# Delta rule scan: right sides solved by halves of a chunk in opposite quadrants, another order of masks, key products and preparation

## The reference

```python
decay = exp(where(tril, gcum[:, None] - gcum[None, :], -inf))
kb    = k * beta[:, None]
lower = where(strict, (kb @ k.T) * decay, 0)
rhs   = concat([v * beta, kb * exp(gcum)], -1)
u, w  = triangular_solve(I + lower, rhs)        # unit lower triangular
attn  = where(tril, (q @ k.T) * decay, 0)
# the state S is carried from chunk to chunk
v_new = u - w @ S
o     = (q * exp(g)) @ S + attn @ v_new
S     = S * exp(g_last) + (k * exp(g_last - g)).T @ v_new
```

## Time and profile before

| what | value |
|---|---|
| median of 3 runs | 4209.52 us (4208.9 to 4209.89) |
| the profiled execution's own time | 4206.61 us |
| its span | 4204.9 us |
| TensorE busy (PE) | 3783.0 us, 90% |
| VectorE busy (DVE) | 2123.8 us, 51% |
| ScalarE busy (ACT) | 870.1 us, 21% |
| GpSimd busy (POOL) | 397.5 us, 9% |

### The profile page before, as it was taken

How to read it: one execution, slowest core, us unless ns; L and a number is a source line. 1 busy time by engine, 2 the same in 40 slices (tenths; PEclk the granted TensorE clock), 3 DMA queues, 4 the chain that set the end, 5 groups by cost and what they waited for, 6 DMA issues and landing times. The chain is left out here.

```text
span 4204.9 us, 67380 instructions
## 1 busy us (share of the span) xinstructions
PE 3783.0 (90%) x28350; PEld 2482.9 (59%) x28350; DVE 2123.8 (51%) x4187; ACT 870.1 (21%) x2114; POOL 397.5 (9%) x506
## 2 busy tenths in 40 slices
PE   6988988995999978889799598897989999999998
PEld 3477467772444435565677243334358878468877
DVE  3777677555222215576646433333364455564455
ACT  3244134411000002251621100002230001441001
POOL 0033013100111110150600000000000000000000
PEclk8999999997999989999999799998999999999999
DMA  6510520026999971211411799994112222122221
GB/s 234 180 38 12 180 92 18 21 81 268 394 393 391 401 260 41 89 54 40 141 61 61 281 404 403 405 421 158 48 66 81 70 90 83 53 81 98 77 90 55
DMA packets 166941, 674.21 MB, mean 160 GB/s; under 512 B 13480, under 2 KB 26984, under 8 KB 142064
## 3 DMA queue, kind: packets, MB, share of 16 engines
q1 hardware_dynamic: 155232, 650.89, 40.6%
q0 software_dynamic: 9984, 16.78, 1.8%
q10 hardware_dynamic: 1424, 2.23, 0.1%
HBM read 652.85 MB, written 17.02 MB: 159 GB/s over the span
## 5 line engine op out<-in xcount | busy, mean ns | idle before, releaser
L3744 PE MATMUL bank<-weight_ring_extra_b,xs_b 128*32 128x512 f32 x2544 | 281.8, 594 | 2.4 <-DMA weight_ring_extra_b<-in_moe_in 2.4
L3744 PE MATMUL bank<-weight_ring,xs_b 128*32 128x512 f32 x1936 | 220.1, 605 | 12.4 <-DVE xs_b L3847 6.2
L2853 PE MATMUL bank<-heads_out_b,swiglu_sums_b 128*128 128x256 f32 x1008 | 224.5, 379 | 0.0
L3836 ACT ACTIVATE moe_silu_b<-bank 128x256 f32<-128x256 f32 x80 | 25.5, 383 | 960.4 <-PE bank L3744 960.4
L3847 DVE TENSOR_SCALAR xs_b<-bank,factor_b,mod_b 128x64 f32<-128x64 f32 (+1 forms) x384 | 95.6, 328 | 229.1 <-PE bank L3728 229.1
L2853 PEld LDWEIGHTS bank<-heads_out_b,swiglu_sums_b 128*128 128x128 f32 x1008 | 191.9, 190 | 25.7
L3744 PEld LDWEIGHTS bank<-weight_ring_extra_b,xs_b 128*32 128x32 f32 x2544 | 79.2, 110 | 178.3 <-issue 173.2
L3801 PE MATMUL bank<-weight_ring_extra_b,moe_hidT_b 128*32 128x256 f32 x2784 | 160.8, 390 | 11.1 <-DMA weight_ring_extra_b<-in_moe_down 9.6
L3888 DVE TENSOR_TENSOR heads_out_b<-heads_out_b,bank 128x256 f32<-128x256 f32 x256 | 90.3, 416 | 154.0 <-PE bank L3781 154.0
L1764 POOL TENSOR_TENSOR d_level_b<-d_low_b,d_mask_b 128x256 f32<-128x256 f32 x144 | 115.5, 830 | 551.1 <-DVE d_far_b L2023 548.2
L2237 PE MATMUL bank<-hT_b,token_block_sums_b 128*128 128x256 f32 x608 | 145.1, 393 | 15.7 <-DVE hT_b L2371 15.7
(11 more groups left out here) (618 smaller groups left out, 7614.2 us busy)
## 6 DMA issues: line engine op xcount, KB each, us to landing
weight_ring_extra_b<-in_moe_in SPq DMA_DIRECT2D x60, 2048.0 KB, 23.4
weight_ring<-in_moe_in SPq DMA_DIRECT2D x48, 2048.0 KB, 24.6
weight_ring_extra_b<-in_moe_down SPq DMA_DIRECT2D x33, 2048.0 KB, 25.2
weight_ring<-in_ada_w SPq DMA_DIRECT2D x24, 2048.0 KB, 8.0
weight_ring<-in_moe_down SPq DMA_DIRECT2D x21, 2048.0 KB, 25.3
weight_ring<-in_ssd_w_in SPq DMA_DIRECT2D x12, 2048.0 KB, 8.2
hT_b<-in_moe_in SPq DMA_DIRECT2D x10, 2048.0 KB, 41.8
weight_ring<-in_ffn_w_gate SPq DMA_DIRECT2D x10, 2048.0 KB, 8.0
```

The source lines that it names most:

```text
L2853: last = pe.matmul(out, lhs[:, k, :], rhs[:, k, :], start=(k == 0), stop=(k == HK - 1))
L3744: last = pe.matmul(in_bank(g)[lanes[c], :], xs[:, e % 2, kt, g * GROUP:(g + 1) * GROUP], w[:, k, :, c * COLS:(c + 1) * COLS], start=(kt == 0),
```

## The change

- Level 64 is dropped. The two 64x64 inverses of a chunk are used directly: the half of the chunk that comes first in a direction's order is solved (`early`), its result is multiplied with `far` (`carry`) and subtracted from the other half's right side (`rest`), and that half is solved (`late`). First half for the forward direction is rows 0 to 63, for the backward one rows 64 to 127, so the products of the two directions lie in opposite quadrants of the array and are issued in turns. Each round is cut in two by heads (r = 0: heads 0 and 2, r = 1: heads 1 and 3).
- After level 32, VectorE's subtraction becomes eight `scalar_tensor_tensor` operations of 128x64, which also multiply with beta, from a copy scaled beforehand (`UB`). The multiplication of `R` with beta and that of `far` with beta are gone. `far` is one buffer whose halves belong to the two directions.
- Keys with queries of the next step go to bank 0 and stand in TensorE's stream before the solve; the transposed keys come after the level-1 transposes and into the same bank. Both Grams of the next step stand after the solve and before the outputs. The outputs go to bank 3, the state sums to bank 2.
- On VectorE both `lower` calls of the next step stand after the forward state and before the backward output. The queries are scaled beside level 8 instead of 16.
- On GpSimd the attention masks stand before the block of level 16 instead of before that of level 4.
- Six more semaphores for the moved products and the preparation.

```diff
@@ order of marks @@
-    PEM = ["gram", "qk", "kturn", "ks", "turn1"]
-    for s in LEVELS[1:]:
+    PEM = ["ks", "turn1", "kturn"]
+    for s in SMALL[1:]:
...
-    PEM += ["new", "o", "state"]
-    BESIDE = {2: ["rest"], 4: ["kend"], 8: ["rb"], 16: ["qs"]}
+    PEM += ["early0", "early1", "carry0", "carry1", "late0", "late1", "o", "state"]
+    BESIDE = {2: ["rest"], 4: ["kend"], 8: ["qs"], 16: ["scaled"]}
@@ GpSimd @@
                 for n, size in enumerate(SMALL):
-                    if n == 2:
+                    if n == 4:
                         attention(s)
@@ TensorE @@
+            def keys_with_queries(d, s):
+                cols = slice(chunk_cols(ORDER[d][s]), chunk_cols(ORDER[d][s]) + P)
+                if s:
+                    wait(pe, dvm[d], s - 1, "kend")
+                else:
+                    wait(pe, acm[d], s, "rowexp")
+                for h in range(GQ):
+                    last = pe.matmul(B[d][0][:, h, :], kT[:, h, cols], qT[:, h, cols], start=True, stop=True)
+                last.then_inc(qk_done[d], 1)
+            def solve(s):
+                for r in range(2):
+                    for d in (FWD, BWD):
+                        wait(pe, dvm[d], s, f"inverse{r}")
+                        wait(pe, dvm[d], s, "rest")
+                    for h in (r, r + 2):
+                        for d in (FWD, BWD):
+                            early, _ = early_late(d)
+                            last = pe.matmul(B[d][1 + r][early, h, :], UW[early, d, 0, h, :], R[early, d, h, :], start=True,
+                                             stop=True)
+                            if h == r + 2:
+                                last.then_inc(pem[d].sem, 1)
...   (carry: far[early] with NW[early] into rows late, after ScalarE's early{r};
...    late: UW[late] with R[late] into rows late, after VectorE's rest{r})
+                if s + 1 < TT:
+                    for d in (FWD, BWD):
+                        keys_with_queries(d, s + 1)
+                solve(s)
+                if s + 1 < TT:
+                    for d in (FWD, BWD):
+                        gram(d, s + 1)
                 for d in (FWD, BWD):
-                    wait(pe, dvm[d], s, "rb")
-                    wait(pe, dvm[d], s, f"uv{TOP}")
-                    each(d, s, "new", B[d][1], lambda h: U[:, d, h, :], lambda h: R[:, d, h, :])
...
+                    for r in range(2):
+                        wait(pe, acm[d], s, f"late{r}")
+                        for h in (r, r + 2):
+                            pe.matmul(B[d][3][:, h, :], QS[:, d, h, :], S[:, d, h, :], start=True, stop=False)
+                            last = pe.matmul(B[d][3][:, h, :], AT[:, d, h, :], NW[:, d, h, :], start=False, stop=True)
                     last.then_inc(pem[d].sem, 1)
-                    each(d, s, "state", B[d][3], lambda h: KE[:, d, h, :], lambda h: NW[:, d, h, :])
-                    if s + 1 < TT:
-                        gram(d, s + 1)
+                    each(d, s, "state", B[d][2], lambda h: KE[:, d, h, :], lambda h: NW[:, d, h, :])
@@ ScalarE @@
+                for n, part in enumerate(("early", "late")):
+                    for r in range(2):
+                        for d in (FWD, BWD):
+                            wait(act, pem[d], s, f"{part}{r}")
+                            if s and n == 0:
+                                wait(act, pem[d], s - 1, "state")
+                            rows = early_late(d)[n]
+                            act.activation(by_two(NW[rows, d])[:, :, r, :], solved_bank(d, r)[rows], ACT.Copy, scale=-1.0) \
+                                .then_inc(acm[d].sem, 1)
@@ VectorE @@
-                dve.tensor_tensor(far[rows], far[rows], beta[rows], ALU.mult).then_inc(dvm[d].sem, 1)
...
+                for r in range(2):
+                    for d in (FWD, BWD):
+                        wait(dve, pem[d], s, f"uv{SMALL[-1]}")
+                        wait(dve, dvm[d], s, "scaled")
+                        for h in (r, r + 2):
+                            at = h0 + h
+                            last = dve.scalar_tensor_tensor(out=UW[:, d, 0, h, :], in0=small_bank(d, 1 + r)[:, h // 2, :],
+                                                            scalar=dec.beta[:, t, d, at:at + 1], in1=UB[:, d, h, :],
+                                                            op0=ALU.mult, op1=ALU.subtract)
+                        last.then_inc(dvm[d].sem, 1)
+                for r in range(2):
+                    for d in (FWD, BWD):
+                        _, late = early_late(d)
+                        wait(dve, pem[d], s, f"carry{r}")
+                        mine = by_two(R[late, d])[:, :, r, :]
+                        dve.tensor_tensor(mine, mine, solved_bank(d, r)[late], ALU.subtract).then_inc(dvm[d].sem, 1)
                 for d in (FWD, BWD):
                     t = ORDER[d][s]
+                    if d == BWD and s + 1 < TT:
+                        for e in (FWD, BWD):
+                            lower(e, s + 1)
                     wait(dve, pem[d], s, "o")
...
-                    if s + 1 < TT:
-                        lower(d, s + 1)
```

More of the change, by code:

```diff
@@ L1781, in turned @@
             def turned(d, s, size):
[L1783 to L1790, removed]
+                for pair in range(GQ // 2):
+                    both = slice(2 * pair, 2 * pair + 2)
+                    last = pe.transpose(small_bank(d, 3)[:, both, :].rearrange("p h c -> p (h c)"),
+                                        UW[:, d, 0, both, :].rearrange("p h c -> p (h c)"), core.ident[:])
                 last.then_inc(pem[d].sem, 1)
@@ L1833, in _ @@
                     cols = slice(chunk_cols(ORDER[d][s]), chunk_cols(ORDER[d][s]) + P)
[L1834 to L1845, removed]
                     if s:
@@ L1856, in _ @@
                     else:
-                        wait(pe, acm[d], s - 1, "new")
+                        wait(pe, acm[d], s - 1, "late0")
                     for h in range(GQ):
@@ L1862, in _ @@
                     last.then_inc(pem[d].sem, 1)
-                for n, size in enumerate(LEVELS):
+                for d in (FWD, BWD):
+                    cols = slice(chunk_cols(ORDER[d][s]), chunk_cols(ORDER[d][s]) + P)
+                    wait(pe, dvm[d], s, "attn")
+                    for h in range(GQ):
+                        last = pe.transpose(B[d][0][:, h, :], kT[:, h, cols], core.ident[:])
+                    last.then_inc(pem[d].sem, 1)
+                for n, size in enumerate(SMALL):
                     if n == 0:
@@ L1870, in _ @@
                             turned(d, s, size)
[L1871 to L1881, removed]
+                        wait(pe, pom[d], s, f"a{size}")
+                        last = (blocks(d, s, small_bank(d, 2), A[:, d, n % 2], UW[:, d, 0]) if n == 1 else
+                                to_places(d, A[:, d, n % 2], UW[:, d, 0]))
                         last.then_inc(pem[d].sem, 1)
@@ L1886, in _ @@
                             wait(pe, dvm[d], s, "uv1")
[L1887 to L1891, removed]
-                        else:
-                            last = (blocks(d, s, small_bank(d, 1), UW[:, d, 1], C[:, d]) if n == 1 else
-                                    from_places(d, UW[:, d, 1], C[:, d]))
@@ L1923, in _ @@
                         wait(act, pom[d], s - 1, "attn")
-                        wait(act, pem[d], s - 1, "new")
+                        wait(act, pem[d], s - 1, "late1")
                     for h in range(GQ):
@@ L2042, in _ @@
                     beside(d, s, 1)
-                for size in LEVELS[1:]:
+                for size in SMALL[1:-1]:
                     for d in (FWD, BWD):
```

137 lines of the change are left out of this document (75 added, 62 removed).

## The result

The changed kernel takes 4289.03 us (median of 4 runs, 4275.54 to 4292.35) against 4209.7 us before (4 runs, 4208.9 to 4211.09): ratio 1.0189, with 95% between 1.0173 and 1.0205. Slower was forecast, and it is slower, but by 79 us and not by 23: the time lies outside the range of 4204 to 4249.

What follows compares the result with a forecast made beforehand. Each scan step was taken as a solve relay, a tail bound by VectorE, and levels with a mask stall. Queue terms of 5.6 us a scan (11.2 for two) plus 12.0 for the clock gave +23.2: 4233 us, range 4204 to 4249.

Steps and rivals of the forecast that it cites:

- both mechanisms that were named: Delta scan: GpSimd's masks hold VectorE's V minus R (+3.68 us a scan); TensorE's clock falls behind long idles (+12.0).
- Solve with Grams: Last level's product to first output product, where the next step's Grams stand ahead of the outputs: 9.0 us.
- idle: Tail: TensorE stands still 3.2 us ahead of keys with the backward state, in each of ten transitions.
- No overlap: Rival, solve: opposite quadrants run one after the other, 0.93 us a half; 4256 us, chance 0.06.
- Not slower: Rival: masks and V minus R don't meet in practice and the clock doesn't fall; 4205 us, chance 0.29.
- Terms of the queues: Delta scan: solve, Grams, tail and levels sum to +5.6 us a scan, +11.2 for two.
- the solve stretch: Last level's product to first output product: 7.20 us against 6.93; about 6.0 in the last step.
- The levels: Start of levels, masks and V minus R taking turns: 6.25 us against 5.78, first step 4.92; +3.68 a scan.
- The tail: First output product to next step's first level product: level products start 0.43 us earlier, -2.1 over five transitions.
- my chain: Solve: rounds begin at 2.92 us, carry at 4.33, late0 at 5.84, output products at 7.20.
- queues only: Rival: the clock never falls, so only the queue terms count; +11.2, 4221 us, chance 0.15.
- the term of the clock: Behind TensorE's ten new idles in the tails, falls to half clock at 1.4 us each: +12.0, bounds 0 and 14.

Runs made afterwards that it cites:

- e8: Changed kernel plus both sets of unread matmuls, 8 in the levels and 24 behind keys-with-state F: 4223.39 us, ratio 1.0033 to the kernel before.
- e1: Changed kernel with the attention masks back in front of level 4's block on GpSimd: 4230.6 us, ratio 1.0046 to the kernel before.
- e3: Changed kernel plus eight unread matmuls in front of level 8's transposes: 4241.49 us, ratio 1.007 to the kernel before.
- e9: Changed kernel with GpSimd's masks waiting for V minus R of both directions, marks reordered: 4233.39 us, ratio 1.0057 to the kernel before.
- e7: Changed kernel plus 24 unread matmuls behind keys-with-state F, filling TensorE's long idle: 4251.57 us, ratio 1.0117 to the kernel before.
- e4: Changed kernel with the next step's preparation back behind each direction's own state sum: 4217.41 us, ratio 1.0013 to the kernel before.
- e2: Kernel before the change, with only the attention masks moved behind level 8's block: 4211.73 us, ratio 1.0005 to the kernel before.
- e10: Changed kernel with preparation back behind each state sum, Grams and key-query products beside VectorE's work, masks behind V minus R: 4195.64 us, ratio 0.9967.
- e5: Changed kernel with masks back before level 4's block and preparation back behind each direction's state sum: 4214.52 us, ratio 1.0023 to the kernel before.

## Why the prediction was wrong in size

**What held.** The direction, both mechanisms that were named, and several sizes. Solve with Grams (287.61 to 297.38) 9.77 us for 8.98; idle 3.14 to 3.57 us for 3.2, ended by the state sum; from level 2's product to level 8's transpose (311.82 to 317.91) 6.09 us for 6.25; V minus R up to 1.76 us for 1.9; 7 of 10 idles followed by a fall, where it was to be eight or nine. Opposite quadrants overlap: eight products of 64x128 take 0.65 us and sixteen 1.09, so one more costs (1.09 - 0.65) / 8 = 0.055 us, half of the 0.111 of the full array. "No overlap" (0.93 for eight) is out. "Not slower" needed the masks not to hold V minus R. They do. (The working says seven idles of 2.9 to 3.6 us at full clock, six with a fall; the trace has an eighth, 3.31 us up to 51.56, with a fall. That changes its 12.0 by 0.3.)

**Terms of the queues: +11.2 forecast, some +19 measured** (e8's scans against those of before; by the ratios +14, with 2 to 26). In e8 the solve stretch is 7.88 us where 7.20 was worked out, and 6.74 in the last step where it was 6.0: 5 x 0.68 + 0.74 = 4.1 a scan. That this is near the whole miss, 9.3 - 5.6 = 3.7 a scan, is luck, for three other differences cancel. The levels came out at +2.1 for +3.7, mostly since the step that was read is the one with 5.78 us and the other four have 5.93 to 5.95. The tail came out at +1.0 for -2.1: 13.28 us for 12.95 where no Gram is made. And the scan's start is 1.8 shorter, since before has the fall of the earlier trace rows there and e8 none; without it the queues' terms would be some +22. Each hand-over between TensorE, ScalarE and VectorE is a little later than my chain had it: early products begin at 3.12 for 2.92, the carry at 4.73 for 4.33, the first late product at 6.40 for 5.84. The rival "queues only", +11, is what e8 shows with +14. It took the two fillers, 8 and 24 unread instructions a step, to bring it about.

**The step that failed: the term of the clock.** "Ten idles of 3.2 [...] 10 x 6/7 x 1.4 = +12.0", with bounds of 0 and 14. Measured: 65.6 us by the ratios (1.0189 - 1.0033 of 4209; by their intervals give or take 14), 51.1 in the profiled execution. Of the latter about 13 are the falls that I priced, 7 of 1.9, where the working had 8.6 of 1.4, 12.0: fewer and dearer, so that the sum agrees better than its parts. The other 8 x 4.4 = 35 to 8 x 4.8 = 38 us are falls in the levels, a term that the working left at nothing. Their cause stood in it, as 5.78 -> 6.25, a wait worth 0.47 us a step; I treated it as time on a queue only and asked about the clock only where TensorE stands still for long, because every fall that I had collected came behind such a standstill, of 2.9 us or more in six cases and, in the earlier trace rows, of 2.02 us by the timeline. The trace of before held no counter-example: its levels are never held up for more than 0.67 us. That absence is a reason for a wide bound, which I didn't give. That the wait is what brings these falls is shown by e1, e3 and e9: one moves the masks, one fills the wait with work, one fixes the order of dispatch, and none leaves a fall in the levels.

The Trainium skill has the rule that I passed over: TensorE: Matmul & The Clock Gate, "A second HAM failure mode: psum-queue depth-cycling", where short idles between groups of matmuls are enough to make the clock swing (HAM is that page's name for the unit that sets the clock; its case is a bf16 kernel with 512 columns). The falls with 1.10 us of wait agree with it, in place of the long idle of its Part 1, on which I leaned alone. On the SBUF interfaces that GpSimd shares with VectorE, the trace agrees with the Trainium skill's GPSIMD Engine Reference, "1. Specifications", which the prediction cites: V minus R takes 0.68 us by itself and 1.25 to 1.76 beside masks.

**Open.** Why 10 of 28 steps with the same 1.1 us of wait keep the clock (281.10 is one). Whether an earlier fall makes one in the levels likelier: it isn't needed (e7), but in the changed kernel a level fall came in 6 of the 7 steps whose long idle was followed by a fall and in none of the 3 whose idle wasn't, and in all 4 first steps of changed and e7; one trace of each is too few to tell. Where the slower executions lose time is not seen either, since one was profiled, but their mean granted clock is on record: the changed kernel's four runs have 0.947 (the profiled one, 4275.54 us), 0.943, 0.942 and 0.940 (4292.35), which by the spans is an estimated 35 to 60 us more at 1.2 GHz than in the profiled one. The kernel before does it too: its 28 runs beside e1 to e4 lie between 4196.92 us at 0.963 and 4231.64 at 0.952. So a count of falls from one trace is a sample.

## What to carry to other kernels

When a change adds a wait to the engine whose clock is governed, price it twice: as time in the queue, and as a chance that what follows runs at half clock. Here 1.1 us of wait was followed by a fall in 18 of 28 steps, and such a fall was worth 4.4 us. Where two engines share an interface, look at who is dispatched first in the step, and fix it with a wait if it matters: here two moves of which neither alone brought more than one or two level falls (e1, e2, e4) brought eight together, because 0.66 us turned that order (the mask 0.56 us ahead, or V minus R 0.1). Then look where the moved work meets the next operation: e9 and e10 lost at level 32 much of what they had won at level 8. If such a clock is suspected, fill the hole with unread products: when more work makes the kernel faster and the granted clock stays up, the clock was it.

## What the runs showed of the hardware that was not expected

- TensorE's clock fell from 2.4 to 1.2 GHz behind a wait of 1.10 us amid transposes and 64x64 products, in 8 of 12 steps of the changed kernel (18 of 28 with waits of 1.09 to 1.28 us over four kernels), in none of 20 with 0.52 to 0.64 us, and stayed low for 10.24 to 17.07 us (20.48 once, e2), though the engine was busy 97% of such a stretch.
- The 20 idles of 1.57 us ahead of full-array products (e4, e5) were followed by no fall, those of 3.14 to 3.57 us by one in 7 (changed), 8 (e1) and 9 (e3, e9) of 10.
- GpSimd's and VectorE's operations with two operands from SBUF hold each other for about the length of an instruction, as if in turns. Alone a subtraction takes 0.68 us and a mask 1.27. When a mask starts 0.56 us ahead, two subtractions take 2.93 and two masks 2.94 (changed); when a subtraction starts 0.1 us ahead, 2.38 and 3.40 (e4); kept apart, 1.30 and 2.51 (e10). Both pairs are done after 3.5 us when they meet and would take 3.8 one after the other.
